# First eight modulation panels in buffers of their own, late bias rows, and one fold for four modulation panels

## What is computed

```python
mod_x = (jax.nn.silu(c) @ w_ada[l] + b_ada[l])[:, None, :]
mod_c = jax.nn.silu(c_ctx) @ w_ada[l] + b_ada[l]
sh1, sc1, g1, shm, scm, gm, sh2, sc2, g2 = jnp.split(mod_x, N_MOD, axis=-1)
h = h + 0.5 * g1 * _swiglu(_modulate(_rms_norm(h, norm_ffn1[l]), sh1, sc1),
                           w_ffn1_gate[l], w_ffn1_up[l], w_ffn1_down[l])
```

## Time and profile before

| what | value |
|---|---|
| median of 3 runs | 2631.45 us (2629.56 to 2631.93) |
| the profiled execution, its own time | 2633.25 us |
| its span in the trace | 2631.9 us |
| TensorE busy, of the span | 93% |
| VectorE, ScalarE, GpSimd busy | 47%, 37%, 17% |
| DMA, mean over the span | 125 GB/s |

### The profile page before, as it was taken

The page is one execution under the profiler, slowest core; times in us unless marked ns, Lnnn a source line. Parts: engine busy times, 40 slices in busy tenths (PEclk is TensorE's granted clock), DMA queues, the critical chain, the costliest instruction groups (busy, mean ns, idle before and its releaser), DMA issues.

```text
span 2631.9 us, 39587 instructions
## 1 busy us (share of the span) xinstructions
PE 2439.9 (93%) x15660; PEld 2007.4 (76%) x15660; DVE 1239.4 (47%) x1910; ACT 966.3 (37%) x1516; POOL 446.3 (17%) x314
## 2 busy tenths in 40 slices
PE   3999999899889999999999998888998799998998
PEld 1677777666567777787888876658987798798988
DVE  1533333445564333334333336566655744776764
ACT  0422221345443222224222224444445333555762
POOL 2000000100000000000000018999995000000000
PEclk9999999999999999999999998988998899999999
DMA  8444445510114444422222241114544222243444
GB/s 254 144 170 171 170 162 189 190 49 32 65 64 160 173 161 155 152 100 89 96 96 81 97 134 56 65 48 144 177 157 145 81 99 73 81 144 145 164 147 137
DMA packets 51154, 330.07 MB, mean 125 GB/s; under 512 B 6048, under 2 KB 7072, under 8 KB 20064
## 3 DMA queue, kind: packets, MB, share of 16 engines
q1 hardware_dynamic: 48560, 318.46, 34.3%
q0 software_dynamic: 2480, 10.01, 1.6%
HBM read 324.64 MB, written 3.80 MB: 125 GB/s over the span
## 4 chain that ended last, share of the span: by engine, by line
PE 80%; DVE 9%; ACT 6%; DMA 2%; issue 2%; ACTq 0%; DVEq 0%; SPq 0%
PE bank L961 23%; PE bank L963 22%; PE bank L962 22%; PE bank L777 3%; DVE wlo L533 2%; DMA raw<-in_stream 2%; PE bank L1547 1%; PE bank L758 1%; ACT whi L531 1%; PE bank L1569 1%; PE bank L1480 1%; PE bank L2077 1%; ACT probs L1517 1%; DVE u_lo L930 1%; ACT probs_t L1554 1%
## 5 line engine op out<-in xcount | busy, mean ns | idle before, releaser
L961 PE MATMUL bank<-u_hi,whi 128*128 128x512 f32 (+1 forms) x2512 | 879.6, 350 | 43.8 <-DVE u_lo L930 25.2
L962 PE MATMUL bank<-u_lo,whi 128*128 128x512 f32 (+1 forms) x2512 | 859.8, 342 | 0.0
L963 PE MATMUL bank<-u_hi,wlo 128*128 128x512 f32 (+1 forms) x2512 | 859.7, 342 | 0.0
L961 PEld LDWEIGHTS bank<-u_hi,whi 128*128 128x128 f32 x2512 | 487.1, 194 | 125.4 <-issue 45.2
L533 DVE TENSOR_TENSOR wlo<-raw,whi 128x2048 fp32r<-128x2048 f32 (+2 forms) x213 | 435.1, 2043 | 294.1 <-ACT whi L531 293.9
L963 PEld LDWEIGHTS bank<-u_hi,wlo 128*128 128x128 f32 x2512 | 486.9, 194 | 51.8
L962 PEld LDWEIGHTS bank<-u_lo,whi 128*128 128x128 f32 x2512 | 488.1, 194 | 48.7 <-issue 0.2
L531 ACT ACTIVATE whi<-raw 128x2048 fp32r<-128x2048 f32 (+2 forms) x213 | 360.9, 1695 | 166.0 <-PE bank L963 124.6
L1023 ACT ACTIVATE sil<-bank 128x512 f32<-128x512 f32 (+1 forms) x88 | 47.9, 544 | 640.2 <-PE bank L963 640.2
L1027 DVE TENSOR_TENSOR prod<-sil,bank 128x512 f32<-128x512 f32 (+1 forms) x88 | 54.7, 621 | 470.7 <-ACT sil L1023 466.8
L1190 POOL DMA_DIRECT2D tables<-in_const x2 | 1.1, 575 | 1510.6 <-PE bank L963 1510.6
(11 more groups left out here) (406 smaller groups left out, 2984.3 us busy)
## 6 DMA issues: line engine op xcount, KB each, us to landing
raw<-in_stream SPq DMA_DIRECT2D x239, 1024.0 KB, 4.8
raw<-in_stream SPq DMA_DIRECT2D x80, 704.0 KB, 4.0
raw<-in_stream SPq DMA_DIRECT2D x8, 768.0 KB, 4.3
skew<-rpb_stage POOLq DMA_DIRECT2D x2, 1344.0 KB, 11.9
nbr_bias<-skew POOLq DMA_DIRECT2D x24, 112.0 KB, 4.6
h<-in_tokens SPq DMA_DIRECT2D x1, 2048.0 KB, 9.8
uq_ukv<-in_small POOLq DMA_DIRECT2D x1, 1536.0 KB, 6.6
tables<-in_const POOLq DMA_DIRECT2D x2, 544.0 KB, 4.0
```

Source lines behind the costliest of these rows:

```text
L961: pe.q.matmul(dst, w[0], x[0], start=start, stop=False)
L962: pe.q.matmul(dst, w[0], x[1], start=False, stop=False)
L963: return pe.q.matmul(dst, w[1], x[0], start=False, stop=stop)
```

## The change

The first eight modulation panels get eight buffers in the arena, a region that later phases use, and a semaphore each, and nothing waits ahead of their loads. SP issues, in this order: `vec`, panels 0 and 1, the tokens, `const`, panels 2 to 5, own panel 0 of `up1`, panels 6 and 7. Then come the other panels as before.

A modulation panel now holds 256 rows of `w_ada` and all 1024 columns of one of the nine vectors, where it held all rows and 256 columns. Four panels accumulate in one PSUM bank. The copy, the fold (with 8 columns instead of 2) and the addition of the bias are done once per four panels, 18 times instead of 72. The fold stands on TensorE ahead of the products of the next four. `down1` carries 14 modulation panels and `down2` 6, where they had 16 and 4. The loop of `up1` and `up2` in the first layer has a body of four groups, and `down2` of the first layer is written out without a loop.

The bias table is read once into 84 rows, and one transfer writes 64 copies of them to DRAM, in pieces of 512 bytes. GpSimd starts this when the eighth modulation panel has been multiplied. `ssq` is cleared by DVE at the very start.

At the start the order on the engines changes too: squares, the split of own panel 0, modulation panels 0 to 5 with the first fold, `norm_scale`, panels 6 and 7, the second fold, the scales, and then `norm`. `norm_scale` no longer waits for the modulation.

What else the diff holds is the removal of code for debugging. Its core:

```diff
--- before.py
+++ after.py
@@ constants
-    c.add("fold", 2)
+    c.add("fold", 8)
-    put("fold", np.stack([(p % 32 == s) for s in range(2)], 1))
+    put("fold", np.stack([(p == 32 * q + s) for q in range(4) for s in range(2)], 1))
+ADA_PART = 4
@@ phases (modulation panels loaded beside each phase)
-        out += [Phase(("up1", l), FC, 16, FC * m), Phase(("down1", l), 16, 11, 16 * m), Phase(("in", l), 9, 16),
-                Phase(("out", l), 4, 16), Phase(("up2", l), FC, 16, FC * m), Phase(("down2", l), 16, 11, 4 * m)]
+        out += [Phase(("up1", l), FC, 16, FC * m), Phase(("down1", l), 16, 11, 14 * m), Phase(("in", l), 9, 16),
+                Phase(("out", l), 4, 16), Phase(("up2", l), FC, 16, FC * m), Phase(("down2", l), 16, 11, 6 * m)]
@@ panel_array
-        return wide(inp["w_ada"][l], slice(None), 256)
+        w = np.asarray(inp["w_ada"][l]).reshape(ADA_PART, 2, P, NMOD, D)
+        return w.transpose(3, 0, 2, 1, 4).reshape(ADA_PANELS, P, ADA_TILES, P)
@@ Stream.__init__: the first eight panels hold no slot
-        for j in range(ADA_FIRST):
-            place("ada", j, j % 2)
+        self.s_first = [nc.alloc_semaphore(f"first_ada_panel_loaded_{j}") for j in range(ADA_FIRST)]
+        for kind in (self.slot, self.there, self.before):
+            kind["ada"] = [None] * ADA_FIRST
@@ Stream.load_all becomes load_first and load_rest
-        for j in range(2):
-            self.load("ada", Count(j), Count(j), 0, ADA_TILES)
-        with self.nc.sync.Fori(0, ADA_FIRST // 2 - 1) as i:
-            for j in range(2):
-                self.load("ada", Count(2 + j, 2, i), Count(2 + j, 2, i), 0, ADA_TILES)
+    def load_first(self, j, dst):
+        size = P * ADA_TILES * P
+        self.nc.sync.dma_start(dst, self.source[j * size:(j + 1) * size].rearrange("(p n) -> p n", p=P))\
+            .then_inc(self.s_first[j], 16)
@@ Stream.run
-        pairs = (n_groups - 4) // 2
-        if loop and pairs >= 2:
+        body = ADA_PART if ph.mod == ph.n and ppg == 1 else 2
+        rounds = (n_groups - 4) // body
+        alike = ph.mod <= 2 * ppg or ph.mod >= (2 + body * rounds) * ppg
+        if loop and rounds >= 2 and alike:
@@ build: the order of the first loads
-    sp.dma_start(const[:, :], ins["const"][:, 0:CC.kept]).then_inc(s_in, 16)
-    sp.dma_start(h[:, :, :], ins["tokens"]).then_inc(s_in, 16)
+    for j in range(2):
+        st.load_first(j, first_ada[j][:, :])
+    sp.dma_start(h[:, :, :], ins["tokens"]).then_inc(s_tok, 16)
+    sp.dma_start(const[:, :], ins["const"][:, 0:CC.kept]).then_inc(s_const, 16)
+    for j in range(2, 6):
+        st.load_first(j, first_ada[j][:, :])
+    st.load("own", Count(0), Count(0), PHASES[0].offset, PHASES[0].tiles)
+    for j in range(6, ADA_FIRST):
+        st.load_first(j, first_ada[j][:, :])
+    st.load_rest()
@@ build: the bias rows
-    stage = [ar.new(f"rpb_stage{l}", [NBR_COLS, rows // L1, SKEW]) for l in range(L1)]
-    zeroed = [pool.do(pool.q.memset(stage[l][:, :, :], 0.0)) for l in range(L1)]
+    stage = sb("rpb_rows", [rows, SKEW])
+    zeroed = pool.do(pool.q.memset(stage[:, :], 0.0))
+    pool.after(zeroed, (st.s_ada, ADA_FIRST))
...
-    for l in range(L1):
-        pool.q.dma_start(flat[:, l, :], stage[l][:, :, :].rearrange("p a b -> p (a b)")).then_inc(s_rpb, 16)
-    pool.q.wait_ge(s_rpb, n_rpb)
-    stage_free = pool.do(pool.q.memset(ssq[:, :], 0.0))
+    pool.q.dma_start(copies, stage[:, :].rearrange("r (o n) -> r o n", o=1).to_broadcast([rows, NBR_COLS, SKEW]))\
+        .then_inc(s_rpb, 16)
+    dve.after(dve.do(dve.q.memset(ssq[:, :], 0.0)))
@@ build: ada_fold and ada_panel
+    def ada_fold(x):
+        pe.q.wait_ge(s_row, x.plus(1))
+        if not x.static() or x.base >= 1:
+            pe.q.wait_ge(s_mod, x.plus(0))
+        for c in range(2):
+            r = pe.q.matmul(banks[7][:, 8 * c:8 * c + 8], row[:, c * P:(c + 1) * P], cst("fold", 8), start=True, stop=True)
+        r.then_inc(s_fold, 1)
...
+    def ada_panel(j, weights=None):
+        k = j.base % ADA_PART
+        x = Count(j.base // ADA_PART, j.step // ADA_PART, j.reg)
...
+        if k == 0 and x.base > ada_done[0]:
+            ada_fold(Count(x.base - 1, x.step, x.reg))
+        for i in range(2):
+            for q in range(4):
+                r = pe.q.matmul(banks[6][32 * q:32 * q + 32, 0:256], csil[:, 2 * k + i, :],
+                                weights[:, i * D + q * 256:i * D + q * 256 + 256],
+                                start=(k == 0 and i == 0), stop=(k == ADA_PART - 1 and i == 1))
+        r.then_inc(st.s_ada, 1)
+        if k == ADA_PART - 1:
+            dve.q.wait_ge(st.s_ada, j.plus(1))
+            if not x.static() or x.base >= 1:
+                dve.q.wait_ge(s_fold, x.plus(0))
+            dve.q.tensor_copy(row, banks[6][:, 0:256]).then_inc(s_row, 1)
@@ build: the order of the start
     for c in range(KC):
         add_square(c, T, last=(c == KC - 1))
     st.split(PHASES[0], Count(0))
+    ada_panels_first(0, ADA_FIRST - 2)
...
+    first_scale = norm_scale(T)
+    ada_panels_first(ADA_FIRST - 2, ADA_FIRST)
+    ada_last(ADA_FIRST - 1)
+    mod_scales(0, 0)
@@ norm_scale
-        pe.after((s_ss, sq_count[0]), loaded, (s_mod, ada_done[0]))
+        pe.after((s_ss, sq_count[0]), loaded)
```

More of the change, by code:

```diff
@@ L487, in load @@
         if before is not None:
-            values = [b and b[1] for b in self.before[kind]]
+            values = [b[1] if b else None for b in self.before[kind]]
             sp.wait_ge(before[0], n.of(values))
@@ L747, in build @@
     diag = sb("inv_norm_diagonal", [P, T])
-    row = [diag[:, 256 * i:256 * i + 256] for i in range(2)]
+    row = diag[:, 0:256]
     ada_done = [0]
-    def ada_fold(j):
-        par = j.base % 2
-        pe.q.wait_ge(s_row, j.plus(1))
-        if not j.static() or j.base >= 2:
-            pe.q.wait_ge(s_mod, j.plus(-1))
-        for c in range(2):
-            x = pe.q.matmul(banks[4 + par][:, 2 * c:2 * c + 2], row[par][:, c * P:(c + 1) * P], cst("fold", 2),
-                            start=True, stop=True)
-        x.then_inc(s_fold, 1)
-        dve.q.wait_ge(s_fold, j.plus(1))
-        at_ = j.times(2).plus(0)
-        bias = vec[:, bass.ds(at_ + VC.at[("b_ada", 0)], 2)].rearrange("p (s c) -> p s c", s=1)
-        dve.q.tensor_tensor(mod[:, :, bass.ds(at_, 2)], banks[4 + par][:, 0:4].rearrange("p (c s) -> p s c", s=2),
-                            bias.to_broadcast([P, 2, 2]), ALU.add).then_inc(s_mod, 1)
@@ L787, in ada_last @@
[L787 to L800 removed]
+    def ada_fold(x):
+        pe.q.wait_ge(s_row, x.plus(1))
+        if not x.static() or x.base >= 1:
+            pe.q.wait_ge(s_mod, x.plus(0))
+        for c in range(2):
+            r = pe.q.matmul(banks[7][:, 8 * c:8 * c + 8], row[:, c * P:(c + 1) * P], cst("fold", 8), start=True, stop=True)
+        r.then_inc(s_fold, 1)
+        dve.q.wait_ge(s_fold, x.plus(1))
+        at_ = x.times(KC).plus(0)
+        bias = vec[:, bass.ds(at_ + VC.at[("b_ada", 0)], KC)].rearrange("p (o q c) -> p o q c", o=1, c=2)
+        dve.q.tensor_tensor(mod[:, :, bass.ds(at_, KC)].rearrange("p s (q c) -> p s q c", c=2),
+                            banks[7][:, 0:16].rearrange("p (c q s) -> p s q c", c=2, q=4),
+                            bias.to_broadcast([P, 2, 4, 2]), ALU.add).then_inc(s_mod, 1)
@@ new lines, in ada_last, with ada_panels_first @@
+    def ada_last(j):
+        if (j + 1) % ADA_PART == 0:
+            ada_fold(Count((j + 1) // ADA_PART - 1))
+        ada_done[0] = (j + 1) // ADA_PART
+    def ada_panels_first(start, end):
+        pe.after((s_vec, 16), c_ready)
+        for j in range(start, end):
+            pe.q.wait_ge(st.s_first[j], 16)
+            if j == ADA_PART:
+                pe.after((s_const, 16))
+                dve.after((s_vec, 16))
+            ada_panel(Count(j), first_ada[j])
+    st.ada, st.ada_last = (lambda j, fold: ada_panel(j)), ada_last
@@ L915, in build, with norm @@
     tmp_free = [None, None]
-    def norm(streams, coeff, then, twice=False):
+    def norm(streams, coeff, then, twice=False, rd=None):
         n = streams * S
-        rd = norm_scale(n, twice, then)
+        rd = rd or norm_scale(n, twice, then)
         scale = banks[4][:, n:2 * n] if twice else banks[4][:, 0:n]
@@ L1610, in build @@
             pass
-        if not reached(("up2", l)):
-            return finish()
         streams = 1 if last else 2
@@ L1618, in build @@
         if l == 0:
-            for n in range(3):
+            for n in range(2):
                 mod_scales(1, n)
```

122 lines of the change are left out of this document (30 added, 92 removed).

## The result

The changed kernel takes 2586.06 us (median of 4 runs, 2583.19 to 2589.67), the kernel before beside it 2631.69 us. The ratio is 0.9827, 95% interval 0.981 to 0.9844. The profiled execution is one of 2588.2 us with a span of 2586.7.

The account below looks back on a forecast made before the run. TensorE was taken to bound the up and down phases with modulation panels, slow successive panel loads the start. Gains of 24.1 (start) and 23.5 (folds), 47.6 us, from 2633.25 leave 2585.7; 1.8 lower for the median: 2584 us, range 2574 to 2604.

Parts of the forecast that it names:

- Own panel 0 was to land at 29.9 us: Start: 10.16 million bytes at 390 GB/s, first byte at 2 us, give 28.0 us; 1.9 added for shared engines.
- 22.5 us from there to the first chunk: Start, from own panel 0's landing: split, copy, folds, products and norm sums at the old pace, 22.1 us plus 0.4 hand-overs.
- The third term: Start of group 1 in up1: no copy and fold stand ahead of its own products any more, worth 0.8 us.
- The step that the first copy waits behind the split: Start: DVE's copy for the first fold queues behind own panel 0's split; the fold and panels 4 and 5 wait.
- part one: The start: first chunk at 52.4 us, 23.3 earlier, plus 0.8 at the first group's end; 24.1 us gained.
- The bias rows: 0 taken, with 0 to 7 as bounds: Near own panel 2's load: the write starts some ten us ahead, in small pieces; 0 cost, otherwise 6 to 7 us late.
- The folds: 23.5 us predicted: TensorE's modulation phases: 47 folds fewer on the path at 0.50 us each, 23.5 us gained (22.1 to 28.7).
- The slower rival: Loops of up1 and up2: each of six jumps fetches three instruction blocks, 11.4 us each; 2652 us, chance 0.03.
- the loop: up1 and up2: the four-group body no longer fits, each of six jumps waits for a block, 23 us; 2607, chance 0.08.
- Slow loads: Start: queue or memory, not the bias table's small pieces, keeps loads at 252 GB/s; gain 9.8 us, 2598 us, chance 0.12.
- free folds: Modulation phases: folds are already hidden, so removing them gives nothing; 2608 us, chance 0.02.
- That TensorE would speed up early: Start: the denser work brings TensorE's faster pace by the norm sums, 5 us more gain; 2579 us, chance 0.2.

Follow-up runs that it names:

- run 6: The changed kernel with the split of own panel 0 emitted behind the first norm scale instead of ahead of modulation panels 0 to 5: 2575.37 us.
- Run 3: The kernel before with only the bias rows changed: compact reads and one write, after the eighth modulation panel, and ssq cleared by DVE: 2614.39 us.
- Run 7: The new start with one fold per modulation panel, and own panel 0's split moved behind the first norm scale: 2609.55 us.
- run 2: The changed kernel with one fold per modulation panel as before, keeping the new loads, buffers, late bias rows and order of the start: 2619.91 us.
- runs 1: The kernel before with only the new folds, weight order and longer loops; start, its buffers and bias rows as before: 2609.0 us.
- Runs 5 and 8: The changed kernel with the bias write once the first eight panels landed, 2578.92 us; the same plus own panel 0's split behind the first scale, 2570.8 us.
- run 5's second kernel: The changed kernel with the bias rows read and written at once, beside the loads of the start: 2583.0 us.

## Why the prediction was right, and where its steps were off

The sign, the mechanism and the size held: 2584 us predicted, 2586.06 measured. Against the terms of the sum, the profiled executions differ by 45.1 us (2633.25 and 2588.2) where 47.6 was forecast. The near hit is partly luck, for three errors cancel: the start gave 5.9 us more than forecast, the folds some 4 less, and the bias rows took 5 that the sum had at nothing.

**The start: 24.1 us predicted, 30.0 measured.** Two terms were mis-sized. Own panel 0 was to land at 29.9 us and landed at 27.3: the loads ran at 416 GB/s, not at the 390 that I took between 370 and 413, and of the 1.9 us added for shared engines 0.9 was needed. (The 9.6 us behind those 1.9 is a slip: 390 GB/s gives 9.2, so the allowance should have been 2.3.) And 22.5 us from there to the first chunk came to 19.1: from the norm sums on the stretch took 9.9 us where the rows of the old start gave 12.6, for TensorE had reached its faster pace (last section). The third term, 0.8 us for the fold that group 1 loses, is right: 29.2 at the first chunk, 30.0 at group 1.

**DVE's queue.** The step that the first copy waits behind the split, with TensorE behind it, is shown by run 6: with the split behind the copy the first chunk comes 8.5 us earlier. The prediction used this to place the first chunk; it did not see it as a fault of the change that a move of one line repairs.

**What the start's gain is made of.** I wrote that GpSimd's transfers no longer share the time, and that the loads came one after the other for want of buffers. Run 3 shows that the first of these is worth 18.8 us of the first chunk's 29.2. Run 7 against run 3 shows 8.8 more for the buffers with their order (56.87 to 48.03), and only with the split moved; run 2 shows less than nothing without that. The four-fold brings another 10.1 (run 6 against run 7), part of it from TensorE's faster pace. The sum did not suffer from this, for part one priced the changed start with its fours; it is the expectation of run 2 that took the two parts as independent, and runs 1 and 2 show that they are not.

**The bias rows: 0 taken, with 0 to 7 as bounds; about 5 measured.** Group 2 came 16.72 us behind group 1, where a period without a fold is 12.15: 4.6 us, of which 3.6 are the wait and 0.9 the slower product behind it. The next group lost another 0.4 (12.59 us). Runs 5 and 8, where the wait is gone, confirm the cause. The step that failed is the reason I gave for taking 0, that the write has a start of some ten us. It had, 53.94 to 64.5, but it took 22.4 us to land, and it slowed a load to 14.04 us, much as the earlier trace rows had shown for the old write (15.5). The bound that came from those rows was right, and the choice within it wrong. The chain names modulation panel 10; own panel 2, which I had named, ended 0.1 us ahead of group 2's products and was as late.

The Trainium skill, page "DMA: Bandwidth & Descriptors", section Specifications, puts pieces of 512 bytes and more at line rate, and by it I had estimated 7 us for the write. The measurement differs where the write ran alone. There the stretch of the changed kernel (columns as in the earlier trace rows) reads:

```profile
58.00:62.00 4.00, 4.00 (x20) 3.23 (x18) 2.08 (x4) 3.95 (x5) 0.00 (x0) 1.00 0.88 205
```

205 GB/s at a DMA share of 0.88, half of the panels' 416 at 1.00. The pieces are 512 bytes by the code (128 words of 4 bytes). But their size is not shown to be the cause. The old write, from 30 to 47 us of the kernel before, is (queue, packets, MB, share of the 16 engines):

```profile
q0 software_dynamic: 160, 2.75, 74.7%
```

Its pieces are 21504 bytes by the code, its packets 17 KB on the mean, and at 162 GB/s for a share of 0.75 it moved no more per share than the new one. Both are writes to DRAM from GpSimd's queue; which part of that slows them, no run here separates. Beside a full queue of loads the new write costs less. In run 5's second kernel writes and loads together moved

```profile
15.00:44.00 29.00, 11.33 (x84) 6.87 (x84) 7.65 (x10) 8.12 (x10) 2.32 (x1) 0.56 0.99 397
```

397 GB/s, not far from the loads' 416 alone.

**The folds: 23.5 us predicted, about 19 measured in the phases.** The products' periods give the price: 0.42 us per fold removed in up1 and up2 and 0.44 in down1, where I had taken 0.50 between 0.47 and 0.61; a new fold costs 0.36 in its place. So both bounds were too high: the period loses less than the 0.47 us from the fold's start to that of the next product. 62 old folds at 0.43 less 14 new ones at 0.36 are 21.6, and 0.8 of that lies in the start's term. Measured are 13.2 from group 2 to the end of down1, 0.4 that the slow group took out of these, 0.4 between groups 1 and 2, and 5.4 in up2 and down2. Some 1.5 us I cannot place. The two panels that moved from the first stretch to the second are why the second gains less per fold.

**The slower rival and the loop.** Neither a block of instructions per jump nor three was fetched. The periods in up1 behind the slow start, and in up2 behind its first group, are 12.14 to 12.15 and 12.50, with no jump to be seen in them. By DMA queue (packets, MB, share), 60 to 112 us and 112 to 280 us of the changed kernel:

```profile
q1 hardware_dynamic: 1210, 8.86, 45.9%
q0 software_dynamic: 561, 2.07, 15.5%
q8 instruction: 3, 0.05, 0.5%
```

```profile
q1 hardware_dynamic: 3904, 28.44, 47.6%
```

Three blocks came while the loop was entered, none in the next 168 us, in which it jumped back; in up2 none came from 820 to 980 us. The rule of the Trainium skill, page "Runtime: NRT & Kernel Launch", section Instruction fetch mechanics, by which a jump outside a window of two blocks stalls, shows nothing here; how many blocks the body of TensorE has, the trace does not tell.

**The other rivals.** Slow loads fall by the 416 GB/s, free folds by run 1. That TensorE would speed up early, which I gave 0.2, happened: by the norm sums, as the rival had it, at a gain of 2.7 us (12.6 to 9.9) instead of 5. The forecast had this at nothing.

**What was to be seen.** The first own product was forecast near 55 us and came at 49.40. The group of bias additions has 18 instructions as forecast:

```profile
L773 DVE TENSOR_TENSOR mod<-bank,vec 128x16 f32 (+1 forms) x18 | 3.0, 169 | 2.0 <-PE bank L768 2.0
```

## What to carry to other kernels

Before giving loads more buffers, look at what else moves in the same stretch: here the side traffic of a small table, many short reads and one write, was 18.8 of the 29.2 us that the first chunk gained. It belongs where no load is waited for, not merely later. In an engine's queue, a small step that others wait for should not stand behind a large one that waits for a load. And two parts of a change that meet on one queue have to be measured apart and together before their gains are added.

## What was not expected of the hardware

In run 6 the records begin at 11.05 us, so there the 16 products of a first panel can be held against them (columns as in the earlier trace rows, then TensorE's timeline):

```profile
22.90:24.00 1.10, 1.10 (x17) 0.43 (x17) 0.17 (x1) 0.00 (x0) 0.00 (x0) 1.00 0.99 410
24.90:26.80 1.90, 1.90 (x17) 0.63 (x17) 0.00 (x0) 0.00 (x0) 0.00 (x0) 0.50 1.01 418
```

```profile
22.94 1.07 PE L789 MATMUL bank<-first_ada,csil 128*32 128x256 f32 x16
24.88 1.93 PE L789 MATMUL bank<-first_ada,csil 128*32 128x256 f32 x16 [0.87 <-DMA first_ada<-in_stream]
```

They take 1.07 us at a granted clock of 1.00 and 1.93 at 0.50, which is the lower of TensorE's two levels, 1.2 GHz. The kernel before needs 1.93 or 1.94 us for a panel's products all through its start, and its own products change their pace at 83 us, where the records begin:

```profile
82.59 0.63 PE L961 MATMUL bank<-u_hi,whi 128*128 128x512 f32 x1
...
83.40 0.40 PE L963 MATMUL bank<-u_hi,wlo 128*128 128x512 f32 x1
```

So it ran its first 83 us at the pace of the lower level, although shows 1.00 there, and "the granted clock reads 1.00 before and behind" in the prediction is a reading of missing records. The changed kernel reached the upper level 46 us earlier, by the norm sums, after TensorE had worked without a wait from 32.08 us on. The fold at 32.08 us takes 1.00 us and that at 45.28 us 0.61 for the same reason.

Behind that the granted clock falls again in the changed kernel. Stretches of it:

```profile
0.00:100.00 100.00, 67.20 (x392) 44.87 (x393) 35.58 (x50) 33.45 (x45) 9.22 (x18) 0.95 0.66 245
...
41.60:44.10 2.50, 2.50 (x25) 1.16 (x28) 0.00 (x0) 0.00 (x0) 0.00 (x0) 0.52 0.00 0
44.10:46.50 2.40, 1.84 (x30) 1.06 (x24) 0.86 (x5) 0.00 (x0) 1.07 (x2) 1.00 0.00 0
...
77.00:80.00 3.00, 1.38 (x16) 0.60 (x16) 1.93 (x1) 2.04 (x3) 0.00 (x0) 0.69 0.02 8
```

0.52 and 0.69 are means that hold some of the upper level. The stretch from 41.60 us lies behind TensorE's wait of 1.29 us ahead of line 916 at 40.10 us. The stretch from 77 us lies behind the 3.6 us in which TensorE waited for modulation panel 10, so that wait cost 0.9 us more in the slow product after it. The mean of 0.95 over the first 100 us counts the unrecorded 37 us as 1.00; it can't be held against the 1.00 that the kernel before shows over the same stretch.
